# Expert loop of a mixture-of-experts step: one expert per round with single buffers, transposes ahead of the down products, a hint for PE's closing branch

## The chip, the cores and the metric

The kernel runs on one core of a Trainium2 chip, in one launch. The metric is the device time in microseconds. PE is the matmul engine (PEld its weight loads), DVE, ACT and POOL the vector, scalar and GpSimd engines, SP the engine that here only issues transfers.

## What is computed

Two layers work on 128 context tokens and 512 latent tokens of width 1024, all in fp32. Each layer has a modulation, an input projection, a convolution and an attention part, an output projection, and then the part that the change touches, an expert-choice mixture:

```python
def expert_choice(h, w_router, w_gate, w_up, w_down):
    B, T, D = h.shape
    C = EC_FACTOR * T // N_EXPERTS
    aff = jax.nn.softmax(jnp.einsum('btd,de->bte', h, w_router).astype(jnp.float32), axis=-1)
    gsel, idx = lax.top_k(aff.transpose(0, 2, 1), C)
    xs = jax.vmap(lambda hb, ib: hb[ib])(h, idx)
    hid = jax.nn.silu(jnp.einsum('becd,edf->becf', xs, w_gate)) * jnp.einsum('becd,edf->becf', xs, w_up)
    ye = jnp.einsum('becf,efd->becd', hid, w_down) * gsel[..., None].astype(h.dtype)
    return jax.vmap(lambda yb, ib: jnp.zeros((T, D), yb.dtype).at[ib.reshape(-1)].add(yb.reshape(-1, D)))(ye, idx)
```

There are 16 experts, each with three 1024x1024 matrices (12.6 MB). Each takes 16 context and 64 latent tokens, 80 rows in all (`CAP`).

## The kernel before

Every engine has its own program, written out by hand, and they meet only at semaphores (`signal`). The layers are unrolled; the 16 experts of a layer are a loop (`Fori`) on PE, DVE, ACT and SP, and unrolled on POOL.

Weights come through a ring of six slots of 2 MB. An expert fills it exactly: units 0 to 3 are the two halves of gate and up, units 4 and 5 the halves of down. SP's loop (L345) issues the refill of a slot with the same unit of the next expert as soon as PE has used the slot (`expert_used`), so a unit has about the time of one expert to land.

For one expert, the steps are these.

- POOL gathers the 80 token rows from `x_unit` in DRAM into `picked` (L1386, an indirect transfer).
- PE transposes them, eight matmuls against the identity (L695, `picked_transposes`), into PSUM. DVE scales and shifts them into `picked_t` (L1265, L1267, `modulate_picked`).
- PE does the gate and up products (L708, `gate_up`), four units of 64 matmuls, with the weights as the stationary side. In the trace each of these fp32 matmuls is two records with two weight loads, so an expert has 512 matmul records of L708.
- ACT takes the SiLU of gate (L924), DVE multiplies with up into `hid` (L1273, `gated_hidden`), once for each half.
- PE does the down products (L722, `down`), 16 matmuls of 512 columns, 32 records. DVE multiplies with the two gates into `added` (L1280, `gated_result`). POOL adds the rows onto `x_res` in DRAM (L1407, an indirect transfer that accumulates), then issues the gather of the expert after the next one.

PE and DVE do two experts a round, so that `picked`, `picked_t` and `added` can have two halves, addressed by constants. PE's round before is:

```python
with pe.Fori(0, EXPERTS // 2) as r:
    picked_transposes(r * 2, 0, r)
    gate_up(r * 2, 0)
    picked_transposes(r * 2 + 1, 1, r)
    down(r * 2)
    gate_up(r * 2 + 1, 1)
    down(r * 2 + 1)
```

The transposes of the second expert stand ahead of the first one's down products. Those of the first expert stand at the head of the round, behind the last down products.

Of the kernel before, what the change touches and what calls it, by code (L numbers as in the profile page):

```python
# [8 lines left out]
D = 1024  # L9
# [14 lines left out]
KD = D // P  # L24
# [43 lines left out]
def build(nc, x_prompt, x_sample, c, cache_k, cache_v, c_ctx, norm1_g, w_mod, b_mod, w_in, conv_w, conv_b,  # L68
# [4 lines left out]
    ALU, ACT = mybir.AluOpType, mybir.ActivationFunctionType  # L73
# [4 lines left out]
    with ctx:  # L78
# [3 lines left out]
        def signal(name, per_layer=0, unit=1):  # L82
            return Signal(ctx.enter_context(nc.semaphore(name)), per_layer, unit)
# [3 lines left out]
        x_unit = nc.dram_tensor("x_unit", (N_TOK, D), f32, kind="Internal").ap()  # L87
# [8 lines left out]
        qk = sb("qk", [P, 2, H, N_TOK])  # L96
        q_t, k_t = qk[:, 0], qk[:, 1]
        qk_flat = qk[:, :, :, :].rearrange("p a h n -> p (a h n)")
        picked = qk_flat[0:CAP, 0:2 * D].rearrange("p (b n) -> p b n", b=2)
        added = qk_flat[0:CAP, 2 * D:4 * D].rearrange("p (b n) -> p b n", b=2)  # L100
        v_sb = sb("v_sb", [P, TILES * BANK])
        v_tok = v_sb[:, :].rearrange("p (t n) -> p t n", t=TILES)
        h2_t = v_sb[:, 0:D].rearrange("p (k n) -> p k n", k=KD)
        picked_t = v_sb[:, D:D + 2 * KD * CAP].rearrange("p (b k n) -> p b k n", b=2, k=KD)
        x_all = qk_flat.rearrange("p (t n) -> p t n", t=TILES)
        mix_flat = mix[:, :, :].rearrange("p k n -> p (k n)")
        hid = mix_flat[:, 0:KD * CAP].rearrange("p (k n) -> p k n", k=KD)
# [25 lines left out]
        ident = sb("ident", [P, P])  # L133
# [41 lines left out]
        row_idx = sb("row_idx", [CAP, EXPERTS], u32)  # L175
        gsel = sb("gsel", [CAP, EXPERTS])
        ps = ctx.enter_context(nc.psum_tensor("ps", [P, 8, BANK], f32))
# [70 lines left out]
        mean_sq2_ready = signal("mean_sq2_ready", TILES)  # L248
        rstd2_ready = signal("rstd2_ready", TILES)

        residual_written = [signal(f"residual_written{b}", 3 - b + EXPERTS // 2, 16) for b in range(2)]
        unit_row_ready = signal("unit_row_ready", TILES)
        unit_stored = signal("unit_stored", TILES, 16)
        x2_transposed = signal("x2_transposed", TILES)
# [9 lines left out]
        top_transposed = signal("top_transposed", 1)  # L264

        result_taken = signal("result_taken", 1 + EXPERTS)
        gathered = [signal(f"gathered{b}", EXPERTS // 2, 16) for b in range(2)]
        picked_transposed = signal("picked_transposed", EXPERTS)
        picked_scaled = signal("picked_scaled", EXPERTS)
        picked_ready = signal("picked_ready", EXPERTS)  # L270
        silu_ready = signal("silu_ready", 2 * EXPERTS)
        hid_ready = signal("hid_ready", 2 * EXPERTS)
        gain_loaded = signal("gain_loaded", unit=16)
# [19 lines left out]
        def tokens(t):  # L293
            return slice(t * P, (t + 1) * P)
# [107 lines left out]
        def _(pe):  # L402
# [64 lines left out]
            for l in range(DEPTH):  # L467
# [221 lines left out]
                pe.wait_ge(*result_taken.at(l, 1))  # L689


                def picked_transposes(e, b, rnd):
                    pe.wait_ge(*gathered[b].at(l, rnd + 1))
                    for k in range(KD):
                        last = nc.tensor.transpose(ps[:, 6 + k // 4, (k % 4) * CAP:(k % 4 + 1) * CAP],  # L695
                                                   picked[:, b, tokens(k)], ident[0:CAP, 0:CAP])
                    last.then_inc(picked_transposed.sem, 1)

                def gate_up(e, b):
                    pe.wait_ge(*picked_ready.at(l, e + 1))  # L700
                    for i in range(4):
                        pe.wait_ge(*expert_loaded[i].at(l, e + 1))
                        w = ring[:, UNIT_SLOTS[l][i], :].rearrange("p (k n) -> p k n", k=KD)
                        for f in range(BLK):
                            for k in range(KD):
                                for c in range(2):
                                    o = f * P + c * HALF
                                    last = nc.tensor.matmul(  # L708
                                        ps[c * HALF:(c + 1) * HALF, i, f * CAP:(f + 1) * CAP], w[:, k, o:o + HALF],
                                        picked_t[:, b, k, :], start=(k == 0), stop=(k == KD - 1))  # L710
                        last.then_inc(expert_used.sem, 1)

                def down(e):
                    pe.wait_ge(*result_taken.at(l, e + 1))
                    for half in range(2):
                        pe.wait_ge(*expert_loaded[4 + half].at(l, e + 1))
                        pe.wait_ge(*hid_ready.at(l, 2 * e + half + 1))
                        w = ring[:, UNIT_SLOTS[l][4 + half], :].rearrange("p (k n) -> p k n", k=KD // 2)
                        for kk in range(KD // 2):
                            k = half * (KD // 2) + kk  # L720
                            for n in range(2):
                                last = nc.tensor.matmul(ps[0:CAP, 4 + n, :], hid[:, k, :],  # L722
                                                        w[:, kk, n * BANK:(n + 1) * BANK],
                                                        start=(k == 0), stop=(k == KD - 1))
                        last.then_inc(expert_used.sem, 1)

                with pe.Fori(0, EXPERTS // 2) as r:
                    picked_transposes(r * 2, 0, r)
                    gate_up(r * 2, 0)
                    picked_transposes(r * 2 + 1, 1, r)  # L730
                    down(r * 2)
                    gate_up(r * 2 + 1, 1)
                    down(r * 2 + 1)


        @block.scalar
# [206 lines left out]
        def _(dve):  # L943
# [39 lines left out]
            for l in range(DEPTH):  # L983
# [272 lines left out]
                dve.wait_ge(*result_taken.at(l, 1))  # L1256


                def modulate_picked(e, b):
                    dve.wait_ge(*picked_transposed.at(l, e + 1))  # L1260
                    dst = picked_t[:, b].rearrange("p (a k) n -> p a k n", a=2)
                    src = ps[:, 6:8, 0:4 * CAP].rearrange("p a (k n) -> p a k n", k=4)
                    sc = scale2_x[:].rearrange("p (a k) n -> p a k n", a=2)
                    sh = shift2_x[:].rearrange("p (a k) n -> p a k n", a=2)
                    nc.vector.tensor_tensor(dst, src, sc, ALU.mult).then_inc(picked_scaled.sem, 1)  # L1265
                    dve.wait_ge(*picked_scaled.at(l, e + 1))
                    nc.vector.tensor_tensor(dst, dst, sh, ALU.add).then_inc(picked_ready.sem, 1)  # L1267
# [6 lines left out]
                                                silu_g[:, half, :].rearrange("p (f n) -> p f n", f=BLK),  # L1274
                                                halves(2 * half + 1), ALU.mult).then_inc(hid_ready.sem, 1)

                def gated_result(e, b, rnd):
                    dve.wait_ge(*expert_used.at(l, e * 6 + 6))
                    dve.wait_ge(*residual_written[b].at(l, rnd + (3 - b)))
                    nc.vector.scalar_tensor_tensor(added[:, b, :], ps[0:CAP, 4:6, :].rearrange("p b n -> p (b n)"),  # L1280
                                                   gsel[:, bass.ds(e, 1)], gate2[:], ALU.mult, ALU.mult)\
                      .then_inc(result_taken.sem, 1)

                with dve.Fori(0, EXPERTS // 2) as r:
                    modulate_picked(r * 2, 0)
                    gated_hidden(r * 2)
                    modulate_picked(r * 2 + 1, 1)
                    gated_result(r * 2, 0, r)
                    gated_hidden(r * 2 + 1)
                    gated_result(r * 2 + 1, 1, r)  # L1290


            gain_rows = h2_t.rearrange("p k n -> p (k n)")
# [11 lines left out]
        def _(pool):  # L1305
# [39 lines left out]
            for l in range(DEPTH):  # L1345
# [34 lines left out]


                def gather(e):
                    b = e % 2
                    if e >= 2:
                        pool.wait_ge(*picked_transposed.at(l, e - 1))
                    nc.gpsimd.indirect_dma_start(  # L1386
                        out=picked[:, b, :], out_offset=None, in_=x_unit,
                        in_offset=bass.IndirectOffsetOnAxis(ap=row_idx[:, e:e + 1], axis=0))\
                      .then_inc(gathered[b].sem, 16)

                pool.wait_ge(*result_taken.at(l, 1))
                pool.wait_ge(*unit_stored.at(l, TILES))
                gather(0)
                gather(1)
                if l == DEPTH - 1:

                    pool.dma_start(h2_t.rearrange("p k n -> p (k n)"),
                                   final_norm_g.rearrange("(a n) -> a n", a=1).to_broadcast([P, D]))\
                        .then_inc(gain_loaded.sem, 16)
                pool.wait_ge(*residual_written[0].at(l, 3))  # L1400
                pool.wait_ge(*residual_written[1].at(l, 2))
                for e in range(EXPERTS):
                    b = e % 2
                    if e > 0:
                        pool.wait_ge(*residual_written[1 - b].at(l, 2 + b + (e + 1) // 2))
                    pool.wait_ge(*result_taken.at(l, e + 2))
                    nc.gpsimd.indirect_dma_start(  # L1407
                        out=x_res, out_offset=bass.IndirectOffsetOnAxis(ap=row_idx[:, e:e + 1], axis=0),
                        in_=added[:, b, :], in_offset=None, compute_op=ALU.add)\
                      .then_inc(residual_written[b].sem, 16)  # L1410
                    if e + 2 < EXPERTS:
                        gather(e + 2)
                pool.wait_ge(*residual_written[1].at(l, 2 + EXPERTS // 2))
                pool.wait_ge(*residual_written[0].at(l, 3 + EXPERTS // 2))

            for t in range(TILES):
                load_x(x_all[:, t, :], DEPTH, t, tile_loaded[t])
# [42 lines left out]
```

## Time and profile before

| what | us |
|---|---|
| median of 3 runs | 2212.54 (2212.06 to 2217.48) |
| the profiled execution's own time | 2215.38 |
| its span, first to last instruction | 2213.3 |
| PE busy with matmuls | 1863.8 (84%) |
| PE busy with weight loads | 1234.8 (56%) |
| DVE / ACT / POOL busy | 634.5 / 310.5 / 127.5 |
| expert loop of layer 0, from its first L708 to the end of its last L722 | 627.6 |
| the same of layer 1 | 608.2 |

The two loops are 1235.8 us of the 2213.3. The busy times add up to more than the span since the engines work side by side; of an engine's idle time only that counts which lies on the chain that ends last. Weight loads overlap matmuls. The mean granted clock of PE is 0.941 of full speed. Of the DMA queues, q1 carries what SP issues (the weights), q0 what POOL issues, q8 and q14 carry instructions.

### The profile page before, as it was taken

The numbers are of one execution on the slowest core, as the hardware profiler recorded it, in microseconds if no ns is written. First come the engines' busy times: TensorE is split into PE (matmuls) and PEld (weight loads), VectorE is DVE, ScalarE is ACT, GpSimd is POOL, SyncE is SP. The second block draws the span as 40 slices with busy tenths as digits, with TensorE's granted clock in tenths as the row PEclk, the third lists the DMA queues.
The fourth block names the chain that finished last, engine by engine and source line by source line (L and its number), as shares of the span: only waits on it lengthen the run. The fifth ranks groups of instructions, "written<-read, shape, count | busy, mean of one in ns | idle before, by whom it ended". The sixth has DMA issues, their size and how long they took to land.

```text
span 2213.3 us, 45747 instructions
## 1 busy us (share of the span) xinstructions
PE 1863.8 (84%) x21107; PEld 1234.8 (56%) x21107; DVE 634.5 (29%) x1040; ACT 310.5 (14%) x616; POOL 127.5 (6%) x155
## 2 busy tenths in 40 slices
PE   4999878959888898888859996888588888898884
PEld 2555455546665665656635553654456665766662
DVE  2089484250100110011020995823300101011011
ACT  3111253210000000000021113522000000000001
POOL 2000000100000000000010000000000000000000
PEclk9999989969999999999979998989799999999997
DMA  9247500539999999999731633033599999999993
GB/s 348 81 152 252 219 14 4 190 129 363 316 344 339 326 344 334 332 333 343 277 129 42 225 133 124 1 114 149 182 340 345 346 359 350 333 349 350 342 339 106
DMA packets 219937, 536.57 MB, mean 242 GB/s; under 512 B 5905, under 2 KB 6322, under 8 KB 219730
## 3 DMA queue, kind: packets, MB, share of 16 engines
q1 hardware_dynamic: 204416, 482.37, 60.6%
q0 software_dynamic: 12128, 41.82, 6.5%
q10 hardware_dynamic: 3186, 9.12, 1.0%
q8 instruction: 191, 3.13, 0.6%
q14 instruction: 16, 0.13, 0.0%
HBM read 508.64 MB, written 24.64 MB: 241 GB/s over the span
## 4 chain that ended last, share of the span: by engine, by line
PE 80%; DVE 8%; issue 7%; DMA 3%; ACT 2%; POOL 0%; DVEq 0%; ACTq 0%; POOLq 0%
PE ps L708 28%; PE ps L722 20%; PE ps L491 13%; PE ps L621 6%; PE ps L503 3%; PE ps L435 2%; DVE neg_m L1114 2%; PE ps L578 1%; PE ps L641 1%; PE ps L444 1%; DMA weight_ring<-in_conv_w_dram 1%; DMA out_dram<-conv_tmp 1%; DVE weight_ring L1150 1%; DVE v_sb L1267 1%; PE ps L695 1%
## 5 line engine op out<-in xcount | busy, mean ns | idle before, releaser
L708 PE MATMUL ps<-v_sb,weight_ring 128*64 128x80 f32 x16384 | 629.2, 241 | 150.5 <-issue 108.4
L708 PEld LDWEIGHTS ps<-v_sb,weight_ring 128*64 128x64 f32 x16384 | 611.5, 143 | 178.5 <-issue 177.6
L722 PE MATMUL ps<-weight_ring,mix 128*80 128x512 f32 x1024 | 445.7, 593 | 0.0
L722 PEld LDWEIGHTS ps<-weight_ring,mix 128*80 128x80 f32 x1024 | 151.0, 150 | 269.5 <-issue 268.0
L491 PE MATMUL ps<-mix,weight_ring 128*128 128x128 f32 (+1 forms) x1024 | 281.1, 435 | 4.9 <-DVE mix L1014 2.7
L491 PEld LDWEIGHTS ps<-mix,weight_ring 128*128 128x128 f32 x1024 | 155.7, 191 | 139.6 <-issue 134.2
L1273 DVE TENSOR_TENSOR mix<-mix,ps 128x320 f32<-128x320 f32 x64 | 31.2, 488 | 703.1 <-PE ps L708 703.1
L1044 DVE SCALAR_TENSOR_TENSOR weight_ring<-u_gate,conv_cols,weight_ring 128x655 f32<-128x655 f32 x240 | 195.1, 892 | 0.0
L924 ACT ACTIVATE mix<-ps 128x320 f32<-128x320 f32 x64 | 28.0, 438 | 1162.8 <-PE ps L708 1162.8
L1280 DVE SCALAR_TENSOR_TENSOR qk<-ps,gsel,gate 80x1024 f32<-80x1024 f32 x32 | 41.0, 1280 | 412.0 <-PE ps L722 412.0
L621 PE MATMUL ps<-weight_ring,mix 128*128 128x512 f32 x320 | 144.6, 608 | 1.9 <-issue 1.9
L1407 POOL DMA_INDIRECT x_res<-qk,row_idx x32 | 45.9, 1435 | 1173.0 <-DVE qk L1280 1102.4
L621 PEld LDWEIGHTS ps<-weight_ring,mix 128*128 128x128 f32 x320 | 61.3, 196 | 74.1 <-issue 74.1
L503 PE MATMUL ps<-weight_ring,mix 128*128 128x512 f32 x160 | 70.5, 596 | 0.0
L846 ACT ACTIVATE weight_ring<-ps,neg_m 128x640 f32<-128x640 f32 (+1 forms) x80 | 55.8, 706 | 2.1 <-DVE neg_m L1114 2.1
L1114 DVE TENSOR_REDUCE neg_m<-ps 128x2 f32<-128x1280 f32 (+1 forms) x40 | 50.8, 1274 | 16.6 <-PE ps L553 16.2
L503 PEld LDWEIGHTS ps<-weight_ring,mix 128*128 128x128 f32 x160 | 29.8, 190 | 40.0 <-issue 40.0
L564 PE MATMUL ps<-ident,weight_ring 128*128 128x128 f32 x168 | 32.9, 300 | 20.5 <-DVE o_tok L1133 10.0
L578 PE MATMUL ps<-v_sb,weight_ring 128*128 128x128 f32 x272 | 45.2, 310 | 4.8 <-ACT weight_ring L864 4.8
L435 PE MATMUL ps<-weight_ring,cond_silu 128*32 128x512 f32 x384 | 47.9, 617 | 0.8 <-issue 0.8
L1026 DVE TENSOR_TENSOR u_gate<-u_gate,conv_tmp 128x128 f32<-128x128 f32 (+1 forms) x16 | 7.2, 489 | 135.7 <-ACT conv_tmp L797 135.7
L578 PEld LDWEIGHTS ps<-v_sb,weight_ring 128*128 128x128 f32 x272 | 37.0, 208 | 11.1 <-ACT weight_ring L864 6.4
(176 smaller groups left out, 1146.2 us busy)
## 6 DMA issues: line engine op xcount, KB each, us to landing
weight_ring<-in_w_gate_dram SPq DMA_DIRECT2D x64, 2048.0 KB, 11.0
weight_ring<-in_w_up_dram SPq DMA_DIRECT2D x64, 2048.0 KB, 10.7
weight_ring<-in_w_down_dram SPq DMA_DIRECT2D x64, 2048.0 KB, 9.7
weight_ring<-in_w_mod_dram SPq DMA_DIRECT2D x24, 2048.0 KB, 8.2
weight_ring<-in_w_in_dram SPq DMA_DIRECT2D x10, 2048.0 KB, 12.1
weight_ring<-in_w_out_dram SPq DMA_DIRECT2D x4, 2048.0 KB, 10.5
x_res<-x_tile POOLq DMA_DIRECT2D x10, 512.0 KB, 3.7
x_unit<-x_norm ACTq DMA_DIRECT2D x10, 512.0 KB, 2.6
```

What stands on the lines that cost most here:

```text
L435: last = nc.tensor.matmul(ps[c * STRIP:(c + 1) * STRIP, 6, :], cond_silu[:, k, :], w[:, k, :], start=(k < 4), stop=(k >= 4))
L491: last = nc.tensor.matmul(ps[:, 2 * (n % 3) + bank, 0:cols.stop - cols.start], w[:, k, tokens(b)], mix[:, k, cols], start=(k == 0), stop=( ...
L503: last = nc.tensor.matmul(ps[:, 2 * (n % 3), :], mix[:, k, tokens(t)], w[:, k, :], start=(k == 0), stop=(k == KD - 1))
L578: last = nc.tensor.matmul(ps[:, 7, tokens(1)], a_col[:, tokens(j)], vals, start=(j == 0), stop=(j == n - 1))
L621: last = nc.tensor.matmul(ps[:, 2 * (i % 2) + n, :], mix[:, k, tokens(t)], w[:, k % 4, n * BANK:(n + 1) * BANK], start=(k == 0), stop=(k = ...
L708: last = nc.tensor.matmul(ps[c * HALF:(c + 1) * HALF, i, f * CAP:(f + 1) * CAP], w[:, k, o:o + HALF], picked_t[:, b, k, :], start=(k == 0) ...
L722: last = nc.tensor.matmul(ps[0:CAP, 4 + n, :], hid[:, k, :], w[:, kk, n * BANK:(n + 1) * BANK], start=(k == 0), stop=(k == KD - 1))
L846: last = nc.scalar.activation(prob[:, b, m, 0:n], score_rows(s)[:, m, :], ACT.Exp, bias=neg_m[:, b, m:m + 1], accum_out=row_sum[:, b, m:m ...
L1044: ins = nc.vector.scalar_tensor_tensor(acc[:, j, :], src, w, acc[:, j, :], ALU.mult, ALU.add)
L1114: nc.vector.tensor_reduce(neg_m[:, s % 2, :], score_rows(s), AX, ALU.max, negate=True)\
L1280: nc.vector.scalar_tensor_tensor(added[:, b, :], ps[0:CAP, 4:6, :].rearrange("p b n -> p (b n)"), gsel[:, bass.ds(e, 1)], gate2[:], ALU.mu ...
L1407: nc.gpsimd.indirect_dma_start(out=x_res, out_offset=bass.IndirectOffsetOnAxis(ap=row_idx[:, e:e + 1], axis=0), in_=added[:, b, :], in_off ...
```

## The change

The round of PE and DVE becomes one expert. `picked`, `picked_t` and `added` keep one half each. The transposes and the modulation of expert 0 move ahead of the loop, and those of expert e+1 stand between the gate and up products and the down products of every expert e. In the last round this makes an unused expert 16, for which POOL gathers the rows of expert 0 once more. POOL's second gather now waits for the first transposes; the scatters all count on `residual_written[0]`. PE's loop gets `hint_back_edge=True`, which puts one more instruction, a hint that names the closing branch, at the head of each round.

```diff
-        picked = qk_flat[0:CAP, 0:2 * D].rearrange("p (b n) -> p b n", b=2)
-        added = qk_flat[0:CAP, 2 * D:4 * D].rearrange("p (b n) -> p b n", b=2)
+        picked = qk_flat[0:CAP, 0:D]
+        added = qk_flat[0:CAP, 2 * D:3 * D]
...
-        picked_t = v_sb[:, D:D + 2 * KD * CAP].rearrange("p (b k n) -> p b k n", b=2, k=KD)
+        picked_t = v_sb[:, D:D + KD * CAP].rearrange("p (k n) -> p k n", k=KD)
...
-                with pe.Fori(0, EXPERTS // 2) as r:
-                    picked_transposes(r * 2, 0, r)
-                    gate_up(r * 2, 0)
-                    picked_transposes(r * 2 + 1, 1, r)
-                    down(r * 2)
-                    gate_up(r * 2 + 1, 1)
-                    down(r * 2 + 1)
+                picked_transposes(0)
+                with nc.Fori(0, EXPERTS, engines=[mybir.EngineType.PE], hint_back_edge=True) as e:
+                    gate_up(e)
+                    picked_transposes(e + 1)
+                    down(e)
...
-                with dve.Fori(0, EXPERTS // 2) as r:
-                    modulate_picked(r * 2, 0)
-                    gated_hidden(r * 2)
-                    modulate_picked(r * 2 + 1, 1)
-                    gated_result(r * 2, 0, r)
-                    gated_hidden(r * 2 + 1)
-                    gated_result(r * 2 + 1, 1, r)
+                modulate_picked(0)
+                with dve.Fori(0, EXPERTS) as e:
+                    gated_hidden(e)
+                    modulate_picked(e + 1)
+                    gated_result(e)
...
                 def gather(e):
-                    b = e % 2
-                    if e >= 2:
-                        pool.wait_ge(*picked_transposed.at(l, e - 1))
+
+                    if e > 0:
+                        pool.wait_ge(*picked_transposed.at(l, e))
+                    at = e % EXPERTS
                     nc.gpsimd.indirect_dma_start(
-                        out=picked[:, b, :], out_offset=None, in_=x_unit,
-                        in_offset=bass.IndirectOffsetOnAxis(ap=row_idx[:, e:e + 1], axis=0))\
-                      .then_inc(gathered[b].sem, 16)
+                        out=picked, out_offset=None, in_=x_unit,
+                        in_offset=bass.IndirectOffsetOnAxis(ap=row_idx[:, at:at + 1], axis=0))\
+                      .then_inc(gathered.sem, 16)
...
                 for e in range(EXPERTS):
-                    b = e % 2
-                    if e > 0:
-                        pool.wait_ge(*residual_written[1 - b].at(l, 2 + b + (e + 1) // 2))
+                    pool.wait_ge(*residual_written[0].at(l, 3 + e))
                     pool.wait_ge(*result_taken.at(l, e + 2))
...
-                    if e + 2 < EXPERTS:
+                    if e + 2 <= EXPERTS:
                         gather(e + 2)
```

On PE the loop's whole round stood as follows before, for its first expert up to the down products of that expert and the head of the second expert. `ps` is PSUM, `qk` holds `picked`, `v_sb` holds `picked_t`, `mix` holds `hid`; 256 matmuls of L708 are four units.

```order
L727 UNCONDITIONAL_BRANCH [waits result_taken]
L727 ISA
L695 MATMUL ps<-ident,qk 128x80 [waits gathered0]
L695 MATMUL ps<-ident,qk 128x80 x7
L700 ISA
L702 REGISTER_ALU [waits picked_ready]
L708 MATMUL ps<-v_sb,weight_ring 64x80 [waits expert_loaded0]
L708 MATMUL ps<-v_sb,weight_ring 64x80 x63
```

Its end, with the down products of the second expert, was this on PE.

```order
L717 ISA [waits expert_loaded4,result_taken]
L722 MATMUL ps<-weight_ring,mix 80x512 [waits hid_ready]
L722 MATMUL ps<-weight_ring,mix 80x512 x7
L717 REGISTER_ALU [waits expert_loaded5]
L722 MATMUL ps<-weight_ring,mix 80x512 [waits hid_ready]
L722 MATMUL ps<-weight_ring,mix 80x512 x7
L727 REGISTER_ALU
L727 COMPARE_AND_BRANCH
```

Now PE's loop is entered behind the first transposes (L728 is the loop's line now).

```order
L695 MATMUL ps<-ident,qk 128x80 [waits gathered,result_taken]
L695 MATMUL ps<-ident,qk 128x80 x7
L728 UNCONDITIONAL_BRANCH
L728 BRANCH_PREFETCH_HINT
L728 ISA
L702 REGISTER_ALU [waits picked_ready]
L708 MATMUL ps<-v_sb,weight_ring 64x80 [waits expert_loaded0]
L708 MATMUL ps<-v_sb,weight_ring 64x80 x63
```

And this is its end on PE, behind the four units of L708.

```order
L693 ISA
L695 MATMUL ps<-ident,qk 128x80 [waits gathered]
L695 MATMUL ps<-ident,qk 128x80 x7
L717 ISA [waits expert_loaded4,result_taken]
L722 MATMUL ps<-weight_ring,mix 80x512 [waits hid_ready]
L722 MATMUL ps<-weight_ring,mix 80x512 x7
L717 REGISTER_ALU [waits expert_loaded5]
L722 MATMUL ps<-weight_ring,mix 80x512 [waits hid_ready]
L722 MATMUL ps<-weight_ring,mix 80x512 x7
L728 REGISTER_ALU
L728 COMPARE_AND_BRANCH
```

What moved: the wait for `picked_ready` in front of L708 now always has the previous expert's down products between it and the transposes that it depends on, and the branch comes after one expert. The program has 560 matmuls in a round before and 280 now.

## Rows read from the trace of the kernel before

**Rows 1.** The page's chain that ended last, shares of the span by line.
```profile
PE ps L708 28%; PE ps L722 20%; PE ps L491 13%; PE ps L621 6%; PE ps L503 3%; PE ps L435 2%; DVE neg_m L1114 2%; PE ps L578 1%; PE ps L641 1%; PE ps L444 1%; DMA weight_ring<-in_conv_w_dram 1%; DMA out_dram<-conv_tmp 1%; DVE weight_ring L1150 1%; DVE v_sb L1267 1%; PE ps L695 1%
```

**Rows 2.** Stretches: length, busy by engine (count), PEclk, DMA share, GB/s.
```profile
484.70:1112.30 627.60, 549.96 (x8824) 395.60 (x8824) 59.25 (x77) 33.26 (x47) 34.26 (x29) 0.96 0.93 328
1574.80:2183.00 608.20, 538.95 (x8824) 385.33 (x8824) 59.25 (x77) 33.25 (x47) 34.45 (x29) 0.97 0.93 328
```

**Rows 3.** PE waits in layer 0's loop, then layer 1's: us, times, longest.
```profile
PE ps L708 <- issue: 58.4, 35, 2.9
PE ps L708 <- DVE v_sb L1267: 21.0, 8, 2.8
...
PE ps L708 <- issue: 49.9, 34, 2.4
```

**Rows 4.** Timeline of PE, first expert of layer 0: start, us, what.
```profile
484.68 20.38 PE L708 MATMUL ps<-v_sb,weight_ring 128*64 128x80 f32 x512 [1.86 <-DVE v_sb L1267]
```

**Rows 5.** The same, later in that loop; in brackets idle before, and releaser.
```profile
543.65 13.96 PE L722 MATMUL ps<-weight_ring,mix 128*80 128x512 f32 x32
...
641.71 7.11 PE L708 MATMUL ps<-v_sb,weight_ring 128*64 128x80 f32 x150 [2.73 <-DVE v_sb L1267]
...
680.19 8.38 PE L708 MATMUL ps<-v_sb,weight_ring 128*64 128x80 f32 x236
690.35 4.65 PE L708 MATMUL ps<-v_sb,weight_ring 128*64 128x80 f32 x128 [1.78 <-issue]
696.82 4.65 PE L708 MATMUL ps<-v_sb,weight_ring 128*64 128x80 f32 x128 [1.82 <-issue]
...
717.93 0.72 PE L695 MATMUL ps<-ident,qk 80*128 80x80 f32 x8
721.38 11.65 PE L708 MATMUL ps<-v_sb,weight_ring 128*64 128x80 f32 x278 [2.73 <-DVE v_sb L1267]
```

**Rows 6.** PE's queue, L727, layers 0 and 1: ns min/median/max, starts.
```profile
L727 PEldq COMPARE_BRANCH  x8: 83/4694/5424, 549.8 to 1104.7; - x8
L727 PEldq COMPARE_BRANCH  x8: 83/6250/6305, 1640.2 to 2175.2; - x8
```

**Rows 7.** DMA queues from 641.7 to 721.4 us: packets, MB, share.
```profile
q8 instruction: 11, 0.18, 0.9%
```

**Rows 8.** DMA view from 1651.3 to 1727.5 us, a round of layer 1.
```profile
DMA packets 10810, 26.59 MB, mean 349 GB/s; under 512 B 253, under 2 KB 253, under 8 KB 10800
q8 instruction: 10, 0.16, 0.9%
```

**Rows 9.** DMA queues from 1148 to 1570 us, between the loops.
```profile
q8 instruction: 13, 0.21, 0.2%
```

**Rows 10.** L1284, the closing branch of DVE's loop, in its queue.
```profile
L1284 DVEq COMPARE_BRANCH  x16: 50/56/67, 557.9 to 2183.3; - x16
```

**Rows 11.** DMA queues from 1574.8 to 2183 us.
```profile
q14 instruction: 1, 0.01, 0.0%
```

**Rows 12.** Stretches as in rows 2: a round, and two slices of 2 us.
```profile
1651.30:1727.50 76.20, 65.81 (x1104) 46.55 (x1104) 7.76 (x10) 4.32 (x6) 4.66 (x5) 1.00 0.99 349
...
693.00:695.00 2.00, 2.00 (x58) 1.83 (x54) 0.00 (x0) 0.00 (x0) 0.00 (x0) 1.00 1.06 388
709.00:711.00 2.00, 2.00 (x6) 0.67 (x5) 0.00 (x0) 0.00 (x0) 0.00 (x0) 1.00 1.06 389
```

**Rows 13.** Timeline of DMA issues, SP's first refill and POOL's.
```profile
491.62 0.39 SPq L345 DMA_DIRECT2D weight_ring<-in_w_gate_dram  x1
...
682.55 1.43 POOL L1407 DMA_INDIRECT x_res<-qk,row_idx  x1 [39.19 <-DVE qk L1280]
684.29 0.92 POOL L1386 DMA_INDIRECT qk<-x_unit,row_idx  x1 [0.30 <-issue]
```

**Rows 14.** DMA issues by line, median us to landing.
```profile
x_res<-qk,row_idx POOLq DMA_INDIRECT x32, 8.3
qk<-x_unit,row_idx POOLq DMA_INDIRECT x32, 8.5
```

More of the change, by code:

```diff
@@ L249, in build @@
         rstd2_ready = signal("rstd2_ready", TILES)
-        residual_written = [signal(f"residual_written{b}", 3 - b + EXPERTS // 2, 16) for b in range(2)]
+        residual_written = [signal("residual_written0", 3 + EXPERTS, 16), signal("residual_written1", 2, 16)]
         unit_row_ready = signal("unit_row_ready", TILES)
@@ L266, in build @@
         result_taken = signal("result_taken", 1 + EXPERTS)
[L267 to L270, printed above, removed]
+        gathered = signal("gathered", EXPERTS + 1, 16)
+        picked_transposed = signal("picked_transposed", EXPERTS + 1)
+        picked_scaled = signal("picked_scaled", EXPERTS + 1)
+        picked_ready = signal("picked_ready", EXPERTS + 1)
         silu_ready = signal("silu_ready", 2 * EXPERTS)
@@ L689, in _, with picked_transposes, gate_up @@
                 pe.wait_ge(*result_taken.at(l, 1))
-                def picked_transposes(e, b, rnd):
-                    pe.wait_ge(*gathered[b].at(l, rnd + 1))
+                def picked_transposes(e):
+                    pe.wait_ge(*gathered.at(l, e + 1))
                     for k in range(KD):
                         last = nc.tensor.transpose(ps[:, 6 + k // 4, (k % 4) * CAP:(k % 4 + 1) * CAP],
-                                                   picked[:, b, tokens(k)], ident[0:CAP, 0:CAP])
+                                                   picked[:, tokens(k)], ident[0:CAP, 0:CAP])
                     last.then_inc(picked_transposed.sem, 1)
-                def gate_up(e, b):
+                def gate_up(e):
                     pe.wait_ge(*picked_ready.at(l, e + 1))
@@ L709, in gate_up @@
                                         ps[c * HALF:(c + 1) * HALF, i, f * CAP:(f + 1) * CAP], w[:, k, o:o + HALF],
-                                        picked_t[:, b, k, :], start=(k == 0), stop=(k == KD - 1))
+                                        picked_t[:, k, :], start=(k == 0), stop=(k == KD - 1))
                         last.then_inc(expert_used.sem, 1)
@@ L1256, in _, with modulate_picked @@
                 dve.wait_ge(*result_taken.at(l, 1))
-                def modulate_picked(e, b):
+                def modulate_picked(e):
                     dve.wait_ge(*picked_transposed.at(l, e + 1))
-                    dst = picked_t[:, b].rearrange("p (a k) n -> p a k n", a=2)
+                    dst = picked_t.rearrange("p (a k) n -> p a k n", a=2)
                     src = ps[:, 6:8, 0:4 * CAP].rearrange("p a (k n) -> p a k n", k=4)
@@ L1275, in gated_hidden, with gated_result @@
                                                 halves(2 * half + 1), ALU.mult).then_inc(hid_ready.sem, 1)
-                def gated_result(e, b, rnd):
+                def gated_result(e):
                     dve.wait_ge(*expert_used.at(l, e * 6 + 6))
-                    dve.wait_ge(*residual_written[b].at(l, rnd + (3 - b)))
-                    nc.vector.scalar_tensor_tensor(added[:, b, :], ps[0:CAP, 4:6, :].rearrange("p b n -> p (b n)"),
+                    dve.wait_ge(*residual_written[0].at(l, e + 3))
+                    nc.vector.scalar_tensor_tensor(added, ps[0:CAP, 4:6, :].rearrange("p b n -> p (b n)"),
                                                    gsel[:, bass.ds(e, 1)], gate2[:], ALU.mult, ALU.mult)\
                       .then_inc(result_taken.sem, 1)
-                with dve.Fori(0, EXPERTS // 2) as r:
-                    modulate_picked(r * 2, 0)
-                    gated_hidden(r * 2)
-                    modulate_picked(r * 2 + 1, 1)
-                    gated_result(r * 2, 0, r)
-                    gated_hidden(r * 2 + 1)
-                    gated_result(r * 2 + 1, 1, r)
+                modulate_picked(0)
[3 more added lines that the diff above has]
+                    gated_result(e)
             gain_rows = h2_t.rearrange("p k n -> p (k n)")
@@ L1393, in _ @@
                 gather(0)
-                gather(1)
                 if l == DEPTH - 1:
@@ L1399, in _ @@
                         .then_inc(gain_loaded.sem, 16)
-                pool.wait_ge(*residual_written[0].at(l, 3))
+                gather(1)
                 pool.wait_ge(*residual_written[1].at(l, 2))
                 for e in range(EXPERTS):
-                    b = e % 2
-                    if e > 0:
-                        pool.wait_ge(*residual_written[1 - b].at(l, 2 + b + (e + 1) // 2))
+                    pool.wait_ge(*residual_written[0].at(l, 3 + e))
                     pool.wait_ge(*result_taken.at(l, e + 2))
@@ L1408, in _ @@
                         out=x_res, out_offset=bass.IndirectOffsetOnAxis(ap=row_idx[:, e:e + 1], axis=0),
-                        in_=added[:, b, :], in_offset=None, compute_op=ALU.add)\
-                      .then_inc(residual_written[b].sem, 16)
-                    if e + 2 < EXPERTS:
+                        in_=added, in_offset=None, compute_op=ALU.add)\
+                      .then_inc(residual_written[0].sem, 16)
+                    if e + 2 <= EXPERTS:
                         gather(e + 2)
-                pool.wait_ge(*residual_written[1].at(l, 2 + EXPERTS // 2))
-                pool.wait_ge(*residual_written[0].at(l, 3 + EXPERTS // 2))
+                pool.wait_ge(*residual_written[0].at(l, 3 + EXPERTS))
             for t in range(TILES):
```

## The prediction

> **What bounds the kernel now.** I read the page's chain of work that ended last first: the two matmul lines of the expert loop, L708 (gate and up) and L722 (down), are 28% and 20% of the span in it [rows 1]. So the case is decided in the 16 experts of each layer. The table of stretches gives these loops 627.6 us in layer 0 and 608.2 us in layer 1, 39.2 and 38.0 us an expert, with PE busy for 550.0 and 539.0 us of them [rows 2]. Everything else (2215.4 - 627.6 - 608.2 = 979.6 us) is left alone by the change.
>
> Then the waits inside the loops. PE is idle before L708 for 58.4 us on "issue" (nothing that the profile shows) in layer 0 and 49.9 us in layer 1, and for 21.0 us in each layer on DVE's L1267 [rows 3]. It never waits for a weight transfer. What is "issue"? The timeline shows the first expert of the loop running its 512 L708 records in 20.38 us without a gap [rows 4]. Later experts are cut into pieces of exactly 128 records, each running 4.65 us, with 1.8 us of nothing behind it: the pieces start at 690.35 and 696.82, 6.47 us apart [rows 5]. 128 is no border of the work (a weight unit is 128 records, but the cuts are at 236, 364 and 492 of an expert's 512). It is a border of the program: 128 matmuls with 128 weight loads are 256 instructions, and queue q8, which carries instructions, moves 11 packets with 0.18 MB in a two-expert round of layer 0, 10 in one of layer 1, and only 13 in 422 us of straight code between the loops [rows 7 to 9]: 16 KB each, 64 bytes for each of 256 instructions. A round has 1104 matmul records, so 2208 instructions and some register ones, 8.7 such blocks. The whole body is therefore fetched again in each round, and the fetch competes with the weights. The same thing shows at the closing branch: it takes 4.7 us (layer 0) and 6.25 us (layer 1) in PE's queue when taken, 0.08 us when it falls through [rows 6]. That one is hidden now, since PE's queue is some 7.7 us ahead of PE: the first branch starts at 549.8 [rows 6], the down products before it run from 543.65 for 13.96 us [rows 5].
>
> **The change, part by part.**
>
> *Single buffers.* `picked`, `picked_t` and `added` lose their second half. The gather for expert e+2 is still issued behind the scatter of e, 4.1 us after the down products end (680.19 [rows 5]; scatter at 682.55, gather at 684.29 [rows 13]), and lands 8.5 us later [rows 14], so 12.6 us into the gate and up products of e+1. Their transposes come at least 18.6 us in. At least 6 us are left: cost nothing; without that cover each us too late costs 16 a layer. `added` is rewritten one expert, over 33 us, after its scatter, which lands in 8.3 us [rows 14]: nothing. Both POOL waits are on transfers issued one expert ago; queued behind them is only POOL's next scatter or gather.
>
> *Transposes ahead of down in every expert.* Now every second expert does transposes, then waits for DVE (L1265, L1267) before L708 can start: from 717.93 to 721.38, 3.4 us [rows 5]. Behind the down products this wait is gone; DVE's modulation (the wait above less the transposes' 0.7 us, under 3 us) lies beside 13.9 us of down products. That takes away the 21.0 us [rows 3]. The clock goes with it: granted clock over the loops is 0.96 and 0.97 [rows 2], and the records after that wait run at the lower level (641.71: 7.11 us for 150, where 128 take 4.65 [rows 5]). PE's clean expert is 512 records at 4.65/128 = 18.6 us, transposes 0.7, down 13.9: **33.2 us**. An extra, unused set of transposes (expert 16) costs 0.7 us a layer, and its modulation lies beside down.
>
> *Half the body, and the hint.* The body becomes 1104 instructions plus 9, 4.35 blocks in place of 8.7. The question on which all hangs: does PE keep a loop of this length, or fetch it again each round? No row shows PE with a shorter loop. DVE's loop of some 28 instructions is kept: its branch takes 56 ns each time [rows 10], and the queue of the other engines' instructions moved one packet in the 608 us of layer 1's loop [rows 11]. PE's of 10 blocks is not. Where the oldest block makes room for the next, a store of any size below 10 would show just the rows seen, so the rows leave all of them open; the new loop touches 5 blocks (layer 1) or 6 (layer 0). Bounds: nothing kept (second case below), or all fetches gone after a layer's first round. The new length is nearer to the long row than to the short one, so by distance I should take "not kept"; I take "kept", because DVE's row shows that an engine looks whether a block is there, and half of a length that fails can be enough. That is a choice, and the chance below says so. The Trainium skill ("Runtime: NRT & Kernel Launch", Instruction fetch mechanics) gives PE 128 KiB of instruction memory, 2048 instructions, in 16 KiB blocks; by that 2221 instructions did not fit and 1113 do, and the sum would be the first case's. The same section, however, calls it a FIFO with purely sequential prefetch and "no instruction cache that benefits from spatial locality", and has a taken branch out of a window of 2 pages wait for its fetch; by that rule the sum would be the second or third case's. The trace agrees with the 16 KB and shows no more of either.
>
> *What comes next once the gaps go.* At 33.2 us PE would ask for 13.3 MB per expert (26.59 MB in a round [rows 8]), 401 GB/s, and no row shows that held. The DMA engines are at a share of 0.99 in that round of 76.2 us already, with 349 GB/s [rows 12]. But 0.99 is not full: in the nine slices from 693 to 711, where several units of weights are queued, the first and the last read 1.06 at 388 and 389 GB/s [rows 12]. With 1.05 as full, an expert costs 0.99 x 38.1 / 1.05 = **35.9 us** of DMA. Lower bound 13.3 MB at 387 GB/s = 34.4; upper bound 0.99 x 38.1 / 1.00 = 37.7. I take 35.9, from the same round and scale, since it keeps the slow moments around gather and scatter. So DMA becomes the bound.
>
> *The sum.* The ring is full on entry. The first refill is issued 6.9 us after L708 begins (491.62 against 484.68 [rows 4, 13]). The DMA then has 90 units of 2 MB (15 experts) to bring, 90 x 35.9/6 = 538.5 us, a first transfer takes about 2 us more than its share, and the last half of down products is 7 us: 554.4 us for a layer. Layer 0: 627.6 to 554.4, -73.2. Layer 1: 608.2 to 554.4, -53.8; its first fetches add perhaps 2. Extra transposes +1.4. Together -123.6. The profiled execution is 2215.4 us and the median of the runs 2212.5, so the change comes to 2091 and **2089 us**. With 34.4 for DMA it is 44 less (2045), with 37.7 it is 54 more (2143).
>
> **The rivals.**
>
> *Fetched as before, hint works (second case).* A crossing then costs 6.47 - 4.65 = 1.8 us of gap. Of the four crossings in an expert's L708 the first is covered (the block behind the branch is asked for while down runs); the second block is asked for as L708 begins, arrives some 6.4 us on and is needed after 149 records, 5.4 us: 1.0; two cost 1.8. 18.6 + 4.6 + 0.7 + 13.9 = 37.8 us. Fifteen experts at 37.8 behind a first one of 35.0 (20.38 + 0.7 + 13.9) are 602 us a layer: -26 and -6, so 2180. For it: no row shows a PE block used twice. Against: DVE's loop.
>
> *Fetched as before, hint without effect: slower.* One mechanism: the closing branch comes after every expert, and behind it gate and up products start at once, where today transposes and the DVE wait cover the fetch of the block after the branch. The queue reaches the branch 7.7 us before down ends, waits 4.7 us, and gets the next block 6.4 us later, 3.5 us after down ended. In layer 0 the loop's head lies near the end of a block (about 21 records of L708 are left in it, 0.8 us), so PE waits 2.7 us, then three times 1.8: 18.6 + 8.1 + 14.6 = 41.3 us against 39.2, +31 in 15 rounds. In layer 1 the built program has 115 records before the first border, so only the three gaps: 38.6 against 38.0, +9. Sum +40: 2252. It decides from the point where branch and next block together take longer than the 7.7 us that PE has queued plus what the head's block gives it.
>
> *DMA is full already.* If 0.99 means full, the loops can only come to 37.7 us: 2143 at best as worked out above, and if more queued weights slow gathers and scatters it gets back to today's 38 to 39: 2195 to 2213, no change. For it: the share. Against: the 388 GB/s.
>
> **How the numbers follow.** Kept, DMA-bound: 0.60, 2089 us, its own range 2045 to 2143. Fetched with a working hint: 0.20, 2180 (2165 to 2195). DMA full already: 0.06. Fetched without hint effect: 0.10, 2252. Else 0.04. The range 2045 to 2192 holds the first case and most of the second. A measurement of this kernel tells 0.3% (7 us) from no change. Faster: 0.60 + 0.19 + 0.04 (DMA full) = 0.83; slower: 0.10 and 0.01 of the rest; same: what is left, 0.06.
>
> **What would show it.** Kept: q8 moves about 6 blocks in a layer's first round and almost none later (some 40 in all, where there are 191 now); the closing branch takes about 0.1 us; L708's "issue" gaps are gone, and waits of L708 on weight_ring transfers stand in their place; 365 GB/s or more over the loops; the clock near 1.00 in them. Fetched: 6 or 7 q8 blocks per expert and gaps every 128 records. No hint effect: branches of 4.7 us or more and a gap 21 records into L708 in layer 0. The size is wrong if the DMA pace is not 35.9: read GB/s in the loop. A wait of L695 on the gather would break the single-buffer term.

## The result and the profile after

The changed kernel takes 2070.15 us (median of 4 runs, 2063.81 to 2072.25) against 2215.01 us for the kernel before (4 runs): a ratio of 0.9338, 95% interval 0.9307 to 0.9368 (the two medians alone give 0.9346). Forecast were 2089 us and a range of 2045 to 2192.

The stretches of the two expert loops in the changed kernel, from the first L708 to the end of the last L722, columns as in [rows 2]; the third row is a part of layer 0's loop:

```profile
490.70:1032.00 541.30, 525.67 (x8832) 373.84 (x8832) 61.21 (x79) 33.23 (x47) 35.18 (x30) 1.00 1.03 375
1495.70:2038.30 542.60, 525.25 (x8832) 373.12 (x8832) 61.23 (x79) 33.23 (x47) 35.37 (x30) 1.00 1.01 367
...
754.60:962.60 208.00, 197.40 (x3313) 139.84 (x3312) 23.44 (x30) 12.94 (x18) 14.04 (x12) 1.00 1.04 382
```

Layer 0's loop went from 627.6 to 541.3 us, layer 1's from 608.2 to 542.6 [rows 2]: 151.9 us less, while the span fell by 145.2 (2213.3 to 2068.1). The other 6.7 us are outside the loops, almost all of it ahead of the first loop, in code that did not change: L708 starts at 490.7 in place of 484.7, and in a later run of the same front part (e1 below) at 496.0. The kernel before, with nothing changed ahead of its loop, starts it at 495.0 in e10. So this is a spread from run to run and no effect of the change; what causes it was not followed. In the loops the granted clock is now 1.00 on average, where it was 0.96 and 0.97; only the first 7 us of layer 0's, behind a wait for the gather and one for DVE, have 0.68.

PE's timeline in the changed kernel, to be held against [rows 4, 5]: two early experts, then one late.

```profile
525.53 17.93 PE L708 MATMUL ps<-v_sb,weight_ring 128*64 128x80 f32 x512
543.39 0.77 PE L695 MATMUL ps<-ident,qk 80*128 80x80 f32 x8
544.00 13.90 PE L722 MATMUL ps<-weight_ring,mix 128*80 128x512 f32 x32
557.83 18.07 PE L708 MATMUL ps<-v_sb,weight_ring 128*64 128x80 f32 x512
...
927.94 13.74 PE L708 MATMUL ps<-v_sb,weight_ring 128*64 128x80 f32 x384
943.45 4.65 PE L708 MATMUL ps<-v_sb,weight_ring 128*64 128x80 f32 x128 [1.77 <-DMA weight_ring<-in_w_up_dram]
948.02 0.77 PE L695 MATMUL ps<-ident,qk 80*128 80x80 f32 x8
948.74 13.96 PE L722 MATMUL ps<-weight_ring,mix 128*80 128x512 f32 x32
962.63 13.75 PE L708 MATMUL ps<-v_sb,weight_ring 128*64 128x80 f32 x384
```

The cuts at 236, 364 and 492 records are gone; L708 follows the down products at once. An early expert takes 32.3 us (525.53 to 557.83). A late one takes 34.7 (927.94 to 962.63), and now the only cut is at record 384, where the fourth unit begins, and its cause is a weight transfer. The first seven experts run at PE's own pace, since the ring is full on entry and the transfers can lag by up to one expert; from then on the transfers set it.

PE's waits in the changed kernel over layer 0's loop (columns as in [rows 3]), where "issue" had 58.4 us and DVE 21.0:

```profile
PE ps L708 <- DMA weight_ring<-in_w_up_dram: 15.5, 9, 1.9
PE ps L708 <- DVE v_sb L1265: 1.9, 1, 1.9
```

The closing branch of PE's loop in the changed kernel, and the DMA queues over 486 us of layer 0's loop (525.5 to 1012). These answer to [rows 6] and [rows 7, 8]:

```profile
L728 PEldq COMPARE_BRANCH  x32: 80/226/264, 517.8 to 2030.5; - x32
```

```profile
DMA packets 75508, 184.41 MB, mean 379 GB/s; under 512 B 1819, under 2 KB 1819, under 8 KB 75508
## 3 DMA queue, kind: packets, MB, share of 16 engines
q1 hardware_dynamic: 72628, 174.58, 96.1%
q0 software_dynamic: 2880, 9.83, 8.1%
```

No q8 line stands there: from the second expert on PE fetches no instructions in this stretch. Over the whole kernel q8 has 35 packets, where it had 191.

### The profile page after: what moved, and what is told of

It reads as the page before. It is cut to its first block, busy times and chain, and to the rows that moved or that the text cites. A ratio compares the mean times of both kernels' runs of the same rounds, so it can differ in the third digit from the quotient of the medians.

```text
span 2068.1 us, 45891 instructions
## 1 busy us (share of the span) xinstructions
PE 1829.5 (88%) x21123; PEld 1202.8 (58%) x21123; DVE 638.8 (31%) x1044; ACT 310.2 (15%) x616; POOL 129.3 (6%) x157
## 4 chain that ended last, share of the span: by engine, by line
PE 66%; DMA 23%; DVE 8%; ACT 1%; issue 1%; POOL 0%; ACTq 0%; DVEq 0%; POOLq 0%
DMA weight_ring<-in_w_up_dram 19%; PE ps L708 16%; PE ps L722 15%; PE ps L491 14%; PE ps L621 7%; PE ps L503 3%; PE ps L435 2%; DVE neg_m L1112 2%; PE ps L695 1%; PE ps L578 1%; PE ps L641 1%; PE ps L444 1%; DMA weight_ring<-in_conv_w_dram 1%; DMA out_dram<-conv_tmp 1%; PE ps L564 1%
## 5 line engine op out<-in xcount | busy, mean ns | idle before, releaser
L708 PE MATMUL ps<-v_sb,weight_ring 128*64 128x80 f32 x16384 | 587.8, 234 | 36.8 <-DMA weight_ring<-in_w_up_dram 30.3
L708 PEld LDWEIGHTS ps<-v_sb,weight_ring 128*64 128x64 f32 x16384 | 577.3, 138 | 66.6 <-DMA weight_ring<-in_w_up_dram 33.2
L722 PE MATMUL ps<-weight_ring,mix 128*80 128x512 f32 x1024 | 445.8, 593 | 0.0
L722 PEld LDWEIGHTS ps<-weight_ring,mix 128*80 128x80 f32 x1024 | 151.0, 150 | 270.0 <-issue 268.0
L1271 DVE TENSOR_TENSOR mix<-mix,ps 128x320 f32<-128x320 f32 x64 | 31.2, 488 | 562.1 <-PE ps L708 562.1
L1171 DVE TENSOR_TENSOR conv_tmp<-ps,u_gate 128x1024 f32<-128x1024 f32 x10 | 12.2, 1225 | 103.5 <-PE ps L621 103.5
```

Of the source, the lines that this page charges most:

```text
L708: last = nc.tensor.matmul(ps[c * HALF:(c + 1) * HALF, i, f * CAP:(f + 1) * CAP], w[:, k, o:o + HALF], picked_t[:, k, :], start=(k == 0), s ...
L722: last = nc.tensor.matmul(ps[0:CAP, 4 + n, :], hid[:, k, :], w[:, kk, n * BANK:(n + 1) * BANK], start=(k == 0), stop=(k == KD - 1))
```

## The experiments

Two theories stood against each other. K: PE keeps a loop that is short enough, and its length is the gain. H: the hint is. A third, M, was that the place of the transposes is all of it. Each ratio is against runs of the kernel before taken beside it (medians 2214 to 2215 us). In the code cuts "..." marks lines left out; lines without a sign are context.

**e1: the hint taken out.**

```diff
-                with nc.Fori(0, EXPERTS, engines=[mybir.EngineType.PE], hint_back_edge=True) as e:
+                with nc.Fori(0, EXPERTS, engines=[mybir.EngineType.PE], hint_back_edge=False) as e:
```

> The changed kernel without the hint; nothing else. Theory K (PE keeps the loop's 5 or 6 instruction blocks, so the target of the branch is there anyway): no difference, 2070 us within 0.3%, about 35 packets on q8, branch 0.1 to 0.3 us. Theory H (the hint brings the blocks in time): the branch waits 4.7 to 6.3 us again, q8 moves 6 or 7 blocks per expert (some 200 in all), time 2180 or more.

2069.66 us (ratio 0.9337, 0.9305 to 0.9370), 36 packets on q8, the branch 0.21 us. The hint does nothing in the changed kernel. H falls for it.

**e2 and e3: two experts in PE's round again, all else as changed**, e2 without the hint, e3 with it.

```diff
-                with nc.Fori(0, EXPERTS, engines=[mybir.EngineType.PE], hint_back_edge=True) as e:
-                    gate_up(e)
-                    picked_transposes(e + 1)
-                    down(e)
+                with nc.Fori(0, EXPERTS // 2, engines=[mybir.EngineType.PE], hint_back_edge=False) as r:
+                    for s in range(2):
+                        gate_up(r * 2 + s)
+                        picked_transposes(r * 2 + s + 1)
+                        down(r * 2 + s)
```

> The changed kernel (single buffers, transposes ahead of down in every expert) with two experts in PE's round in place of one, no hint. Only the length of PE's loop differs from e1: 2221 instructions, 8.7 blocks. Theory K: the blocks are fetched again, 10 or 11 a round, gaps of 1.8 us return in L708, about 37.8 us an expert, 2165 to 2185 us. Theory M (the gain comes from moving the transposes, not from the loop's length): 2070 us as e1.

> As e2 with the hint on the closing branch. Theory K: the hint shortens the branch's 4.7 to 6.3 us to about 0.1 to 2 us and saves the useless block past the loop's end (one q8 packet a round fewer), but that wait lay beside down anyway, so within 1% of e2. Theory H: near 2070 us.

e2: 2206.83 us (0.9954, 0.9934 to 0.9974), q8 199 packets. e3: 2158.76 us (0.9738, 0.9695 to 0.9781), q8 187. So the same instructions in the same order, with a loop of 2221 in place of 1112, cost 137 us: M falls, the length is the gain (with the hint on both sides, e3 against the changed kernel, it is 89 us). e2 came out 22 us above the upper end that K gave it (2185): the experts behind the branch cost more than the 37.8 us assumed. And my expectation of e3 was wrong: with the longer loop the hint is worth 48 us. PE's timeline shows where. First e2, then e3, each from behind the branch:

```profile
717.48 1.04 PE L708 MATMUL ps<-v_sb,weight_ring 128*64 128x80 f32 x22
720.64 4.65 PE L708 MATMUL ps<-v_sb,weight_ring 128*64 128x80 f32 x128 [2.12 <-issue]
727.39 4.65 PE L708 MATMUL ps<-v_sb,weight_ring 128*64 128x80 f32 x128 [2.10 <-issue]
```

```profile
712.25 10.03 PE L708 MATMUL ps<-v_sb,weight_ring 128*64 128x80 f32 x278
723.26 4.65 PE L708 MATMUL ps<-v_sb,weight_ring 128*64 128x80 f32 x128 [0.98 <-issue]
```

Without the hint the queue stands at the branch (5.15 us in the median, 0.49 with it), and the block after it comes that much later. The branch itself lies beside the down products, but PE then meets the end of the head's block 22 records into L708, and waits 2.1 us there and 2.1 at the next border; with the hint 278 records run through and the wait is 0.98. This is the mechanism of my third rival; I had left it out of e3's expectation.

**e4: one expert a round, but the transposes at the head of the round.** The edit is shown against e1, the changed kernel without the hint.

```diff
-                picked_transposes(0)
                 with nc.Fori(0, EXPERTS, engines=[mybir.EngineType.PE], hint_back_edge=False) as e:
+                    picked_transposes(e)
                     gate_up(e)
-                    picked_transposes(e + 1)
                     down(e)
```

(DVE's `modulate_picked` moves likewise, and expert 16 is gone.)

> One expert a round, single buffers, no hint, but the transposes of every expert at the head of its round, behind the last down products. Loop length as e1. Every expert then has the wait for DVE (2.75 us and the transposes' own 0.7) and the records at the lower clock after it (about 1.7 us): 18.2 + 0.7 + 2.8 + 1.7 + 13.9 = 37.3 us, against 34.7 by the transfers in e1; 2.6 us x 30 = +78: 2148 us. Blocks kept, q8 about 35. Theory M, in which the place of the transposes is all of the gain, expects 2210 us or more.

2131.67 us (0.9610, 0.9566 to 0.9653), q8 36. PE's timeline of e4:

```profile
812.92 0.72 PE L695 MATMUL ps<-ident,qk 80*128 80x80 f32 x8
816.29 17.93 PE L708 MATMUL ps<-v_sb,weight_ring 128*64 128x80 f32 x512 [2.65 <-DVE v_sb L1264]
834.15 13.96 PE L722 MATMUL ps<-weight_ring,mix 128*80 128x512 f32 x32
847.95 0.72 PE L695 MATMUL ps<-ident,qk 80*128 80x80 f32 x8
851.32 19.57 PE L708 MATMUL ps<-v_sb,weight_ring 128*64 128x80 f32 x512 [2.65 <-DVE v_sb L1264]
```

An expert takes 35.0 and 36.7 us in turn, since the records at the lower clock come only behind every second such wait (17.93 against 19.57 us; granted clock 1.00 in the 4 us behind 816.3, 0.61 in those behind 851.3); I had charged them to every expert, and expected 2148 us. Where the loop is kept, the place of the transposes is worth 62 us (2131.67 - 2069.66), with 30 of 32 waits for DVE taken away. With the long loop what it is worth hangs on the hint. Without one it is about 8 us (2215.32 for the kernel before, 2206.83 for e2), since waits for blocks come up where the wait for DVE was. With one it is 57 us (2215.73 in e10 below, 2158.76 in e3). These two pairs also differ in the single buffers, and take away 14 waits, not 30.

**e5 to e7: how many blocks does PE keep?** Two experts a round, the loop's head put on the first slot of a 16 KB block, and all but 4 of the 64 L708 matmuls of one unit (e5, e6) or of one unit of each expert (e7) left out. That makes loops of 1981 and 1741 instructions: 7.7 and 6.8 blocks, 8 and 7 touched. e6 is e5 with the hint.

```diff
...
+                with nc.Fori(0, EXPERTS // 2, engines=[mybir.EngineType.PE],
+                             head_slot={mybir.EngineType.PE: 0}, hint_back_edge=False) as r:
+                    for s in range(2):
+                        gate_up(r * 2 + s, [i for t, i in [(0, 3)] if t == s])
...
```

> Two experts a round without hint, with one of the round's eight gate/up units left out of the computation (all but 4 of its 64 matmuls of L708; its transfer stays), so the loop has 1981 instructions, 7.7 blocks, and its head put on the first slot of a block: 8 blocks touched. If PE's store holds 8 blocks and the block past the loop's end is still fetched each round (a 9th): oldest goes first, all 9 are fetched again, q8 about 9 x 16 + 25 = 170. If the store holds 9: q8 about 40. If it holds 6 or 7: also about 170, and e7 tells.

> As e5 with the hint, same work left out. If the hint takes the fetch of the block past the end away, 8 blocks are asked for in a round: kept with a store of 8, q8 about 45, no gaps in L708, faster than e5 by 50 us or more. If the store is smaller than 8, or the hint does not take that fetch away: as e5.

> Two experts a round without hint, one unit of each expert left out of the computation (transfers stay): 1741 instructions, 6.8 blocks, 7 touched and 1 past the end, 8 in all. With a store of 8 blocks: kept, q8 about 45, no gaps. With 7 or fewer: about 8 x 16 + 25 = 150 packets.

The q8 line and the branch of e5, of e6 and of e7 (two of the 18 branches stand at the entries of the two loops):

```profile
q8 instruction: 169, 2.77, 0.5%
...
L728 PEldq COMPARE_BRANCH  x18: 79/6234/6292, 490.9 to 2071.3; - x18
```

```profile
q8 instruction: 43, 0.70, 0.1%
...
L728 PEldq COMPARE_BRANCH  x18: 80/223/322, 487.6 to 2030.3; - x18
```

```profile
q8 instruction: 41, 0.67, 0.1%
...
L728 PEldq COMPARE_BRANCH  x18: 76/208/317, 491.6 to 2038.5; - x18
```

One run each: 2111.04, 2070.39 and 2077.88 us. Of e7's 41 packets 27 lie outside the loops (14 up to 480 us, 13 from 1040 to 1490) and 7 in each loop (480 to 1040, 1490 to 2040); e6 has 8 in each. With the same 27 outside, e5's 169 leave 8.9 a round, so that nearly all of nine blocks come again each time. This is what a store of 8 blocks gives in which the oldest makes room. A loop of 8 blocks asks for a ninth, the one past its end, and loses all (e5). The hint takes that request away, and the same loop is kept (e6, 41 us less, where I had expected 50 or more). A loop of 7 is kept without a hint (e7). The packet counts carry this reading, not the single times.

**e8 and e9: half of each down unit not transferred**, e8 on the changed kernel, e9 on the kernel before.

```diff
...
+                if i >= 4:
+                    dst, src = dst[:, 0:2, :], src[:, 0:2, :]
...
```

> The changed kernel with only half of each down unit transferred (1 MB in place of 2 for units 4 and 5; the computation runs on, partly on old data): 10.5 MB of weights an expert. If transfers bound the changed loop at 34.7 us, PE bounds it now at 32.4 to 33.2 us an expert: 15 x 1.5 to 2.3 us a layer less, 2001 to 2025 us. If PE is the bound already, 2070.

> The kernel before with the same half of the down units left out of the transfers. If the gaps are the instruction fetch queued behind weights, they shrink where fewer weights are under way but stay where gate and up units are being refilled: L708 issue gaps from 108 us to 50 to 90 us, 2150 to 2195 us. If the gaps are a fixed latency of the fetch, they stay at about 108 us and the time at 2212.

e8: 2031.69 us (0.9191, 0.9162 to 0.9221). Layer 0's loop in e8, and PE's waits in e9's loops (the edit adds four lines, so that L708 is L712 and DVE's L1267 is L1271 there):

```profile
489.20:1012.40 523.20, 522.57 (x8832) 372.13 (x8832) 61.21 (x79) 33.26 (x47) 35.25 (x30) 1.00 0.97 332
```

```profile
PE ps L712 <- issue: 64.2, 48, 2.4
PE ps L712 <- DVE v_sb L1271: 42.0, 16, 2.8
```

PE is busy for 522.6 of 523.2 us, 32.7 us an expert. So in the changed kernel the transfers are the bound and cost 38 us over both layers; I had expected 45 to 69 us. e9: 2157.84 us (0.9768, 0.9729 to 0.9807), inside the 2150 to 2195 expected. With the same program and the same 191 packets on q8, the "issue" gaps fall from 108.4 us in 69 to 64.2 in 48, while the wait for DVE stays at 42.0: a fetch takes longer the more weights are under way, and its lateness is no fixed latency.

**e10: the kernel before with the hint alone.**

```diff
-                with pe.Fori(0, EXPERTS // 2) as r:
+                with nc.Fori(0, EXPERTS // 2, engines=[mybir.EngineType.PE], hint_back_edge=True) as r:
```

> The kernel before with the hint alone; buffers, order and the two experts a round stay. 9 or 10 blocks are still asked for in a round, more than the 8 that e5 to e7 show to be kept, so all are fetched again: q8 about 175 to 191. The branch's wait goes, but it lies beside down; the block after the branch arrives about 4.7 us sooner, which the transposes and the wait for DVE cover today. So only the crossing after it gains, 0 to 1.5 us a round: 2190 to 2215 us. If the hint were worth here what it is between e2 and e3 (48 us): 2167.

2215.73 us (1.0008, 0.9990 to 1.0025), q8 179 packets, the branch 0.45 us in the median in place of 5.42. The 12 blocks saved in 16 rounds and the short branch gain nothing. At the first border behind the branch PE waits 0.77 us (layer 0, from 657.87) where the kernel before waits 0.44 (649.26): the reading that fits is that transposes and the wait for DVE, which stand behind the branch there, cover its wait already. e2 does not have this cover.

## Why the prediction came out as it did

- *"PE keeps a loop of this length"* (0.60) was right, and was a choice: the rows gave no length. The closing branch takes 0.23 us, not the 0.1 of a branch to a kept block that I had written. e5 to e7 put the border at 8 blocks; the old round of 9 or 10 and its follower were past it, the new one of 5 or 6 is well inside. The Trainium skill ("Runtime: NRT & Kernel Launch", Instruction fetch mechanics) has 128 KiB for PE in 16 KiB blocks, which makes 8: e5 to e7 agree with the number. The same section says that there is "no instruction cache that benefits from spatial locality"; if that means that a loop's blocks are never used again, it does not hold on PE here: 35 packets in place of 191. The measurement decides.
- *The gaps every 128 records are instruction fetches*: right; they went with q8's packets.
- *DVE's wait and the low clock go*: right, 1.9 us of it is left in a layer (the first expert) and the clock is 1.00. e4, which has such a wait in every expert, is 62 us slower than e1.
- *PE's clean expert, 33.2 us*: 32.3 measured early in the loop. An uncut L708 takes 17.9 to 18.2 us, not the 18.6 that pieces of 128 gave, since a record lasts 0.23 us while the next starts 0.035 us behind it, and each piece ends with a whole last record.
- *"DMA becomes the bound"*: right. *35.9 us an expert* is the term that was mis-sized: 34.7 measured. I scaled a round's rate by its share and called what was slow in it moments around gathers and scatters. The share came out as assumed, 1.04 for 1.05, but a share of 1.00 carried 353 GB/s in that round (349/0.99) and 367 late in the changed loop (382/1.04). The deepest moment of that round was no gather either:

```profile
1689.00:1691.00 2.00, 2.00 (x66) 2.00 (x62) 1.24 (x1) 0.00 (x0) 0.00 (x0) 1.00 0.29 84
```

  It lies ahead of POOL's scatter, which is issued at 1691.02. In that round SP issues the refills one by one, 4 to 8 us apart, as PE frees the slots (1668.51, 1674.32, then two from 1681.89), so the likely cause is that too little was queued. In the changed kernel no slice of 2 us from 928 to 964 has a share under 1.01. Behind a scatter and gather (930.31, 932.04) the rate still falls, to 309 GB/s, and is over 400 afterwards:

```profile
936.00:938.00 2.00, 2.00 (x65) 2.00 (x62) 0.49 (x1) 0.00 (x0) 0.00 (x0) 1.00 1.05 309
950.00:952.00 2.00, 2.00 (x6) 0.75 (x5) 0.52 (x1) 0.00 (x0) 0.00 (x0) 1.00 1.01 406
```

  90 units at 34.7/6 make 520.5 in place of 538.5 us, 18 us less a layer.
- *The sum*, 554.4 us a layer, was 541.3 and 542.6. With 34.7 it gives 536.4; of the 5 to 6 us missing 3 would be the lower rate of the first experts (376 GB/s from 525.5 to 720.3), an estimate that was not tried by itself, and the rest stays open. The 19 us between 2089 and 2070 add up as follows. The loops took 24.9 less, and the 3.4 that I had added for first fetches and extra transposes did not come on top: 28.3. Against that stand 6.7 more outside the loops, and the 3 us that I had taken off between the profiled run and the median, which the changed kernel does not show (2069.92 and 2070.15).
- *Single buffers cost nothing*: right, L695 waits for a gather only in the first expert of a layer.
- *The fetched rivals*: the mechanism of the third, the branch's wait and then the next block, is the one seen in e2. Its size can't be checked at one expert a round, since that loop is kept. In e2 only every second expert has the branch ahead of it: 40.9 us in layer 0 (717.48 to 758.33) and 40.2 in layer 1 (1645.48 to 1685.73), where 41.3 and 38.6 were forecast; with the experts between them the means are 39.0 and 37.9.
- *Hint*: it was in the sum at nothing in the first case; e1 agrees. e10 agrees too.

## What to carry to other kernels

Where an engine shows idle time on nothing at equal numbers of instructions, count instructions, not work: look at the queue that carries them, and ask how many blocks a round of the loop touches. On PE a round of up to 7 blocks of 256 (8 with a hint) is fetched once; one more block and all of it comes again in each round, past the weights. Before shortening a wait, see which other wait lies behind it: moving the transposes gave about 8 us in the long loop, 57 in the long loop with a hint and 62 in the short one. And a full ring hides a transfer bound for a while (seven experts here), so read the pace late in a loop.

## What the runs showed of the hardware

- PE keeps 8 blocks of 16 KB; the block past a loop's closing branch counts as one more (8 touched: 169 packets in e5; 7 touched: 41 in e7), unless the branch is hinted (8 touched: 43 in e6).
- With the transfers as the bound, SP's issue of a 2 MB transfer takes 5 to 10 us in its queue, where it took 0.37. The changed kernel's SP:

```profile
905.46 10.08 SPq L345 DMA_DIRECT2D weight_ring<-in_w_up_dram  x1
915.80 4.96 SPq L345 DMA_DIRECT2D weight_ring<-in_w_gate_dram  x1
920.94 5.16 SPq L345 DMA_DIRECT2D weight_ring<-in_w_up_dram  x1
```

- Gathers and scatters are not slower for it: 7.5 us to landing, where [rows 14] have 8.5 and 8.3.
- After the same idle time of 2.65 us before L708, the records behind it run at the lower clock only every second time from the third expert on (e4: 19.57 and 17.93 us for 512 records; the second and third experts both have 19.57).
